# Odd attention: probabilities times values in three passes of high and low parts, for the second half of the queries and heads 0 to 6

## The chip, the cores and the metric

The kernel runs on one core of a Trainium2 chip. The metric is the time of the whole program on the device, in microseconds (us). The engines are PE (TensorE), DVE (VectorE), ACT (ScalarE), POOL (GpSimd) and SP (SyncE, which issues the DMAs). Each runs its own queue of instructions in order and waits for the others through semaphores.

## What is computed

Three transformer layers in float32 over 1024 rows of width 1024. The change is in the second one, the odd layer: an index score keeps at most 256 keys for each query, and 8 heads with 128 columns each (heads 0 to 3 share one set of keys and values, 4 to 7 the other) attend to them:

```python
def dsa_attention(q, k, v, qi, ki, wi, rel_bias):
    ...
        _, idx = lax.top_k(score, topk)
        ...
        logits = jnp.einsum('bqhgd,bqkhd->bqhgk', q_blk, k_sel) * (Dh ** -0.5)
        logits = jnp.where(valid[:, :, None, None, :], logits + bias, NEG_INF)
        p = jax.nn.softmax(logits, axis=-1).astype(v.dtype)
        return jnp.einsum('bqhgk,bqkhd->bqhgd', p, v_sel)

def odd_layer(hn, rel_bias, w_in, w_out, q_g, k_g):
    ...
    att = dsa_attention(q, k, v, qi, ki, wi, rel_bias)
    return (att * jax.nn.silu(gate)) @ w_out
```

The kernel gathers nothing: it computes all logits up to the diagonal and adds a mask of 0 and -1e30.

## The kernel before

All large products are made from parts. A float32 tile x has a high part, x rounded to the type float32r by an ACT copy (`act_panel`, `act_parts`), and a low part, x minus the high one, by a subtraction on POOL or DVE. `mm3` issues three matmuls: high by high, high by low, low by high. Products that are not split are one plain float32 matmul (`mm`); the trace records each of these as two.

The odd layer goes in this order: projections (`qi`, `ki`, `ok`, `ov`, `oq`), the search for the 256th score on DVE and ACT, the eight gate projections `og0` to `og7` with the norms of the heads beside them, then the attention, then the product with `w_out` (`oo`). Weights come in panels of 128 x 1024: SP loads one into one of two raw buffers, ACT makes the high part in one of four slots (8 KB for high and low together), POOL the low part. Panel i+2 is loaded when panel i is split. Before the attention four `oo` panels (oo000 to oo003) are split, one behind each of og4 to og7, and two more lie in the raw buffers.

The attention has 64 units (n, b): head n, query block b of 128 rows with b+1 key blocks. One loop on each engine runs over steps i with shifted stages:

- `s0` on POOL (L2568) adds the bias strip of the head to the mask for b of 2 and more, into one of two tiles by the parity of b. It waits for `od_L` of two blocks earlier.
- `s1` on PE makes the logits (3 or 6 matmuls), DVE (L2318, recorded as CUSTOM_DVE) adds the bias and takes the row minimum of the negated sum (`od_L`), ACT (L2501) takes the exponential with its row sum (`od_exp`).
- `s2`, two steps later: PE turns the 128 x 128 blocks (L267) into a bank of the ring `od_ptb`, up to four blocks a bank, so one bank for b of 0 to 3 and two for b of 4 to 7. A copy moves each bank to the tile `pts[Q]`, where Q is 0 for b below 4 and 1 from 4 on. For b = 4 to 6 ACT (L2510) copies the first bank and DVE (L2333) the second; for b = 7 DVE copies both. The copy frees the bank. The ring has three banks, and each turn needs the bank of three turns ago.
- `s3`, four steps after b = 3 or 7: PE spreads the reciprocals of the row sums (4 matmuls) into a bank of the same ring, then multiplies the values `VN` (stationary) by `pts[Q]` into bank 3. DVE (L2341, L2344) multiplies by reciprocals and gate, ACT (L445) makes the high part of the result and POOL (L2573) the low one.

While a head's Q = 1 probabilities are turned, PE and DVE already work on b = 0 to 3 of the next head: in the order of every engine, the logits, the minimum and the exponential of the next head's b = 0 stand between the copies of b = 5 and of b = 6, and those of b = 1 between b = 6 and b = 7. POOL also makes the low parts of the next head's queries (`query_low`, L2551) at b = 5 and 6. The work around attention's end is: SP waits for the end marks of all engines, reads back the residual of 4 MB and three rows of parameters, and goes on with the panels.

In the kernel, `at` names the semaphore value of an event and `up` raises it.

Of the kernel before, what the change touches and what calls it, by code (L numbers as in the profile page):

```python
# [161 lines left out]
class K:  # L162
# [3 lines left out]
    def __init__(self, nc, d, known):  # L166
# [1656 lines left out]
class Odd:  # L1823


    def __init__(self, k, E):
# [126 lines left out]
def tensor_odd(k, O):  # L1953
# [145 lines left out]
    def s3(n, Q):  # L2099
# [12 lines left out]
        else:  # L2112
            pe.wait_ge(*at("od_g", *before((n, Q), 1, 2)))
        kv, last = n // 4, 4 * Q + 3
        for j in range(last + 1):
            q0 = max(0, j - 4 * Q)
            ins = k.mm(k.bank(3)[:, 128 * q0:512], O.VN[:, j, 128 * kv:128 * kv + 128],
                       O.pts[Q][:, j, q0:4, :].rearrange("p q s -> p (q s)"), j == 0, j == last)
        ins.then_inc(*up("od_O", n, Q))
# [29 lines left out]
def vector_odd(k, O):  # L2149
# [175 lines left out]
    def s2(n, b):  # L2325
        for j0 in range(0, b + 1, 4):
            if j0 == 0 and b % 4 != 3:
                continue
            nj = min(4, b + 1 - j0)
            dve.wait_ge(*at("od_PT_ps", n, b, j0))  # L2330
# [43 lines left out]
def scalar_odd(k, O):  # L2374
# [104 lines left out]
    for m in range(8):  # L2479
        for half in range(2):  # L2480
# [5 lines left out]
            if m >= 2:  # L2486
                act.wait_ge(*at("og_out", m - 2))
            A.activation(O.gev[m % 2][:, 512 * half:512 * half + 512], k.bank(O.proj[("og", m, half)]), ACT.Silu).then_inc(
                *up("og", m, half, also=[("free", "od_proj", "og", m, half)]))
        act_panel(k, PANEL_AT[f"og{m}"] + 4)  # L2490
        if m == 3:
# [10 lines left out]

    def s2(n, b):
        if b % 4 == 3:
            return
# [12 lines left out]
    for i in range(len(O.units) + 4):  # L2518
# [8 lines left out]
        if i < len(O.units) and O.units[i] == (1, 4):  # L2527
            key_high(1)
    k.mark("od_att")
    scalar_out(k, "oo", k.H, "ln0", lambda: act_transposes(k, k.second.x0, "xs", None, (0,)), lambda: k.marks(act, "od_att"))  # L2530
# [3 lines left out]
def pool_odd(k, O):  # L2534
# [13 lines left out]
    def query_low(n, half):  # L2548
        o = slice(512 * half, 512 * half + 512)
        pool.wait_ge(*at("od_qh", n))  # L2550
        G.tensor_tensor(O.QL[:, n, o], O.QT[:, n, o], O.qh[n % 2][:, o].bitcast(F32), ALU.subtract).then_inc(*up("od_ql", n, half))  # L2551

    for name in panels[:-1]:
        pool_panel(k, PANEL_AT[name] + 4)
        if name in ("og4", "og5"):
            key_low(0, int(name == "og5"))
        if name == "og6":
            query_low(0, 0)
            query_low(0, 1)
# [15 lines left out]
    for i in range(4):  # L2575
        s0(*O.units[i])
    pool_panel(k, PANEL_AT[panels[-1]] + 4)
    for i in range(len(O.units) + 7):
        if 4 <= i + 1 < len(O.units):
            s0(*O.units[i + 1])  # L2580
# [13 lines left out]
def sync_odd(k, O):  # L2594
# [37 lines left out]
    for m in range(8):  # L2632
        if m < 7:
            sp_panel(k, PANEL_AT[f"og{m}"] + 6)
        sp.wait_ge(*at("og", m, 1))
        S.dma_start(d["gscr"][128 * m:128 * m + 128], O.gev[m % 2]).then_inc(*up(f"og_out{m % 2}", by=16, also=[("og_out", m)]))
    load_strip(1)
    sp.wait_ge(*at("og_ps", 7, 1))
    load_gate(0)
    sp_panel(k, PANEL_AT["og7"] + 6)  # L2640
    for n, b in O.units:
        if 0 < n < 7 and b == 0:
            load_strip(n + 1)
        if n < 7 and b == 5:
            load_gate(n + 1)
    k.marks(sp, "od_att")
    for t in range(2):
# [1328 lines left out]
```

## Time and profile before

| | us |
|---|---|
| median of three timed runs | 1995.52 (1995.45 to 1996.81) |
| the profiled execution | 1991.9 |
| its span in the trace | 1990.6 |
| attention in the trace, from the first logits to the last product | 810 to 979 |

The profile has a page of totals, and views of the trace: groups of instructions by line and form, waits, a timeline, and busy time in stretches. A record's time is from start to end; matmuls overlap, so their rate is read from the distance between starts or from a count in a stretch. What stands in square brackets behind a record is the idle time of the engine before it and the instruction that ended it.

### The profile page before, as it was taken

To read this page: it belongs to the slowest core of one execution; us is meant where nothing else is said; L and a number is where in the kernel's file an instruction comes from. 1 tells how busy PE (TensorE), PEld (TensorE's weight loads), DVE (VectorE), ACT (ScalarE), POOL (GpSimd) and SP (SyncE) were. 2 spreads that over 40 slices of the span, in tenths; PEclk is the share of its full clock that TensorE was granted. 3 is DMA by queue.
4 is the path that set the end of the run, shared out by engine and by line. 5 is a ranking of instruction groups with operands and counts; after the bars stand their busy time and mean duration, and the time that the engine had idled before them with its cause. 6 is when DMAs were issued, how large, how long until landed. Compare 5 with 4: busy or idle time off the path is not lost.

```text
span 1990.6 us, 24260 instructions
## 1 busy us (share of the span) xinstructions
PE 1924.6 (97%) x9188; PEld 1511.5 (76%) x9188; DVE 1423.6 (72%) x2190; ACT 862.2 (43%) x1457; POOL 640.1 (32%) x453
## 2 busy tenths in 40 slices
PE   7999989999999999999999999999999999999997
PEld 6778766787648787777788777888787877777886
DVE  7668776523279998455356799899999877685549
ACT  5343385333356862555312333444225554352431
POOL 3554410462201222676454000000003663236444
PEclk9999999999999999999999999999999999999999
DMA  7322340442511122211233211121123223455322
GB/s 274 126 74 79 100 146 22 169 149 81 140 35 33 43 85 85 85 65 43 104 119 117 75 39 58 53 64 53 64 97 131 90 75 143 159 193 203 109 91 108
DMA packets 72429, 197.92 MB, mean 99 GB/s; under 512 B 11182, under 2 KB 20559, under 8 KB 71800
## 3 DMA queue, kind: packets, MB, share of 16 engines
q1 hardware_dynamic: 72168, 196.36, 28.9%
q8 instruction: 73, 1.20, 0.2%
q14 instruction: 44, 0.36, 0.1%
q10 hardware_dynamic: 144, 0.00, 0.0%
HBM read 152.90 MB, written 46.71 MB: 100 GB/s over the span
## 4 chain that ended last, share of the span: by engine, by line
PE 54%; DVE 25%; ACT 4%; issue 3%; DMA 1%; POOL 1%; SPq 0%; DVEq 0%; ACTq 0%
PE psum L264 50%; DVE m L3031 6%; DVE m L2194 4%; PE psum L267 3%; DVE m L3052 2%; DVE m L319 1%; DMA m<-in_w 1%; DVE m L3233 1%; ACT m L299 1%; DVE m L532 1%; DVE m L541 1%; DVE m L3170 1%; POOL m L309 1%; DVE m L2263 0%; DVE m L404 0%
## 5 line engine op out<-in xcount | busy, mean ns | idle before, releaser
L264 PE MATMUL psum<-m,m 128*128 128x512 f32 (+8 forms) x8388 | 1844.4, 389 | 38.1 <-DVE m L319 10.0
L264 PEld LDWEIGHTS psum<-m,m 128*128 128x128 f32 (+4 forms) x8388 | 1427.0, 186 | 429.3 <-issue 118.8
L309 POOL TENSOR_TENSOR m<-m,m 128x1024 fp32r<-128x1024 f32 (+1 forms) x122 | 308.6, 2533 | 1003.8 <-ACT m L299 1003.5
L299 ACT ACTIVATE m<-m 128x1024 fp32r<-128x1024 f32 (+2 forms) x166 | 173.6, 1049 | 356.4 <-PE psum L264 228.5
L3031 DVE SCALAR_TENSOR_TENSOR m<-m,m,m 128x1024 f32<-128x1024 f32 x240 | 311.0, 1297 | 6.3
L267 PE MATMUL psum<-m,m 128*128 128x128 f32 x784 | 112.4, 278 | 15.9 <-ACT m L1451 6.2
L267 PEld LDWEIGHTS psum<-m,m 128*128 128x128 f32 x784 | 88.7, 141 | 33.0 <-ACT m L1451 8.2
L2194 DVE TENSOR_SCALAR_CACHE_REDUCE m<-m,m 128x896 bf16<-128x896 f32 (+4 forms) x130 | 102.8, 848 | 1.1
L2568 POOL TENSOR_TENSOR m<-m,m 128x384 f32<-128x384 f32 (+5 forms) x48 | 72.8, 1532 | 43.2 <-DVE m L2318 43.1
L2318 DVE CUSTOM_DVE_ANT_0 m<-psum,m 128x128 f32<-128x128 f32 (+3 forms) x64 | 48.3, 755 | 40.0 <-PE psum L264 22.0
L2414 ACT ACTIVATE m<-m,m 128x1024 bf16<-128x1024 f32 (+1 forms) x62 | 64.1, 1036 | 26.4 <-DVE m L2221 26.4
L319 DVE TENSOR_TENSOR m<-m,m 128x1024 fp32r<-128x1024 f32 (+1 forms) x44 | 52.7, 1198 | 26.0 <-ACT m L299 26.0
L2501 ACT ACTIVATE m<-m,m 128x128 f32<-128x128 f32 (+3 forms) x64 | 49.5, 773 | 37.3 <-DVE m L2318 37.0
L483 DVE TENSOR_TENSOR m<-psum,m 128x512 f32<-128x512 f32 x32 | 21.6, 682 | 60.7 <-PE psum L264 53.9
L2173 DVE SCALAR_TENSOR_TENSOR m<-m,m,m 128x512 f32<-128x512 f32 (+3 forms) x70 | 48.9, 706 | 17.6 <-ACT m L2464 12.9
L2464 ACT ACTIVATE m<-psum 128x512 f32<-128x512 f32 (+3 forms) x80 | 37.7, 522 | 30.2 <-PE psum L264 25.5
L467 POOL TENSOR_TENSOR m<-m,m 128x1 f32<-128x1 f32 x23 | 31.5, 1373 | 50.6 <-DVE m L460 50.6
L3052 DVE SCALAR_TENSOR_TENSOR m<-m,m,m 128x1024 f32<-128x1024 f32 x36 | 46.2, 1283 | 0.9
L404 DVE SCALAR_TENSOR_TENSOR m<-psum,m 128x512 fp32r<-128x512 f32 x32 | 19.7, 681 | 34.1 <-ACT m L393 34.0
L404 DVE SCALAR_TENSOR_TENSOR m<-psum,m,m 128x512 fp32r<-128x512 f32 x32 | 21.6, 743 | 30.8 <-ACT m L393 30.8
L1264 DVE TENSOR_TENSOR m<-psum,m 128x512 f32<-128x512 f32 x16 | 11.0, 689 | 43.3 <-PE psum L264 43.3
L541 DVE SCALAR_TENSOR_TENSOR m<-m,m,m 128x1024 f32<-128x1024 f32 (+1 forms) x25 | 36.8, 1494 | 6.8 <-POOL m L467 6.6
(319 smaller groups left out, 1612.2 us busy)
## 6 DMA issues: line engine op xcount, KB each, us to landing
m<-in_w SPq DMA_DIRECT2D x164, 512.0 KB, 3.5
scr_hscr<-m SPq DMA_DIRECT2D x4, 2048.0 KB, 6.7
m<-scr_hscr SPq DMA_DIRECT2D x4, 2048.0 KB, 10.7
scr_turned<-scr_strip SPq DMA_DIRECT2D x8, 575.5 KB, 13.0
m<-in_x SPq DMA_DIRECT2D x4, 1024.0 KB, 8.1
scr_gscr<-m SPq DMA_DIRECT2D x16, 256.0 KB, 4.2
m<-in_x SPq DMA_DIRECT2D x2, 2048.0 KB, 7.9
m<-scr_turned SPq DMA_DIRECT2D x8, 512.0 KB, 4.5
```

The source lines that it names most:

```text
L264: return self.nc.tensor.matmul(out, lhsT, rhs, start=start, stop=stop, skip_group_check=True)
L267: return self.nc.tensor.transpose(out, in_, self.ident[:, :])
L299: k.nc.scalar.activation(k.hi[SLOT[i]][:, 0:kk * n], k.raw[i % 2][:, 0:kk * n], ACT.Copy).then_inc(*k.up("w_hi", i))
L309: k.nc.gpsimd.tensor_tensor(lo, raw, hi.bitcast(F32), ALU.subtract).then_inc(*k.up("w_lo", i))
L319: k.nc.vector.tensor_tensor(lo, raw, hi.bitcast(F32), ALU.subtract).then_inc(*k.up("w_lo", i))
L541: k.nc.vector.scalar_tensor_tensor(x[:, b, cols], x[:, b, cols], scale, shift[:, cols], ALU.mult, ALU.add).then_inc(*k.up(f"{name}_y", b, ...
L2194: V.tensor_scalar(O.JK[b], O.SC[b], TF[:, c:c + 1] if i else 0.0, None, how, ALU.add, accum_out=CNT[:, c:c + 1]).then_inc(*up("count", i, b))
L2414: A.activation(O.JK[b], O.SC[b], ACT.Sign, bias=O.TB.bitcast(F32)[:, c:c + 1] if i else 0.0, accum_out=O.CNT[:, c:c + 1]).then_inc(*up("si ...
L2501: A.activation(p, p, ACT.Exp, bias=sm[:, 0:1], scale=-1.0, accum_out=O.sums[b // 4][:, b % 4:b % 4 + 1]).then_inc(*up("od_exp", n, b))
L2568: G.tensor_tensor(O.bms[b % 2][:, 0:nk], O.strips[n % 2][:, 1024 - nk:1024], O.MK[:, O.mo[b]:O.mo[b] + nk], ALU.add).then_inc(*up("od_bm", ...
L3031: V.scalar_tensor_tensor(o, u[:, j:j + 1024], w[:, j:j + 1], o, ALU.mult, ALU.add).then_inc(*up("cv_tap", m, j))
L3052: V.scalar_tensor_tensor(o, x[:, j:j + 1024], cw[:, j:j + 1], o, ALU.mult, ALU.add).then_inc(*up("xb_tap", i, j))
```

## The change

For Q = 1 and n below 7 (`parted`), the product of probabilities and values is made by `mm3` from high and low parts in place of one float32 matmul for each key block. For n = 7, and for Q = 0 everywhere, nothing changes.

- Probabilities: for these 28 units ACT copies both banks into a high tile `PTH`, and DVE subtracts that from the same bank into low tiles `PTL`. A bank is free when DVE's subtraction is done.
- Values: ACT makes `VH` in two instructions behind og4's second gate half, POOL makes `VL` in two, one before `query_low` of head 0 and one after the first two bias tiles.
- `VH`, `VL` and the two `PTL` tiles lie in the four weight slots (8 KB each). So the panels oo000 to oo003 are no longer split before the attention. ACT splits them in steps 60, 61, 66 and 67, POOL in steps 63, 64, 66 and 68, and SP loads oo002 to oo005 at the end of the attention, before the residual.

```diff
+        self.PTH = k.tile(X0 + 8 * KB, [8, 4, 128], F32R)
+        slot = [k.slots[SLOT[PANEL_AT[f"oo00{i}"]]] for i in range(4)]
+        self.VH, self.VL = (k.tile(o, [8, 256], F32R) for o in slot[0:2])
+        self.PTL = [k.tile(o, [4, 4, 128], F32R) for o in slot[2:4]]
+        self.parted = lambda n, Q: Q == 1 and n < 7
...
+        if O.parted(n, Q):
+            pe.wait_ge(*at("od_vl"))
         for j in range(last + 1):
...
+            if O.parted(n, Q):
+                parts = (x[:, i, q0:4, :].rearrange("p q s -> p (q s)") for x, i in ((O.PTH, j), (O.PTL[j // 4], j % 4)))
+                ins = k.mm3(out, (O.VH[:, j, hs], O.VL[:, j, hs]), tuple(parts), j == 0, j == last)
+            else:
+                ins = k.mm(out, O.VN[:, j, hs], O.pts[Q][:, j, q0:4, :].rearrange("p q s -> p (q s)"), j == 0, j == last)
...
     def s2(n, b):
         for j0 in range(0, b + 1, 4):
+            nj = min(4, b + 1 - j0)
+            if O.parted(n, b // 4):
+                dve.wait_ge(*at("od_PT_high", n, b, j0))
+                V.tensor_tensor(O.PTL[j0 // 4][:, 0:nj, b % 4, :], k.bank(O.ptb[("PT", n, b, j0)])[:, 0:128 * nj].rearrange("p (j q) -> p j q", j=nj),
+                                O.PTH[:, j0:j0 + nj, b % 4, :].bitcast(F32), ALU.subtract).then_inc(
+                    *up("od_PT_low", n, b, j0, also=[("od_PT", n, b, j0), ("free", "od_ptb", "PT", n, b, j0)]))
+                continue
...
-        act_panel(k, PANEL_AT[f"og{m}"] + 4)
+        if m < 4:
+            act_panel(k, PANEL_AT[f"og{m}"] + 4)
+        if m == 4:
+            act.wait_ge(*at(*done("og4")))
+            for q in range(2):
+                A.activation(O.VH[:, 4 * q:4 * q + 4, :], O.VN[:, 4 * q:4 * q + 4, :], ACT.Copy).then_inc(*up("od_vh", q))
...
+        if O.parted(n, b // 4):
+            for j0 in (0, 4):
+                nj = min(4, b + 1 - j0)
+                act.wait_ge(*at("od_PT_ps", n, b, j0))
+                if n:
+                    act.wait_ge(*at("od_O", n - 1, 1))
+                A.activation(O.PTH[:, j0:j0 + nj, b % 4, :], k.bank(O.ptb[("PT", n, b, j0)])[:, 0:128 * nj].rearrange("p (j q) -> p j q", j=nj), ACT.Copy).then_inc(
+                    *up("od_PT_high", n, b, j0))
+            return
...
+        if i in (60, 61, 66, 67):
+            act.wait_ge(*at("od_O", 6, 1))
+            act_panel(k, PANEL_AT["oo000"] + (60, 61, 66, 67).index(i))
...
+    def value_low(q):
+        b = slice(4 * q, 4 * q + 4)
+        pool.wait_ge(*at(*done("og5")))
+        pool.wait_ge(*at("od_vh", q))
+        G.tensor_tensor(O.VL[:, b, :], O.VN[:, b, :], O.VH[:, b, :].bitcast(F32), ALU.subtract).then_inc(*up("od_vl", "part", q, also=[("od_vl",)] if q else ()))
...
+        if i in (63, 64, 66, 68):
+            pool_panel(k, PANEL_AT["oo000"] + (63, 64, 66, 68).index(i))
```

ACT's order in the attention, from b = 7's exponential of head 3 to the next head's b = 2. m_194 to m_196 hold probabilities, m_198 is `pts[1]`, 128x4x128 is a bank with four blocks. Before:

```order
L2501 ACTIVATE m_196,m_61<-m_196,m_61 128x1024
L2510 ACTIVATE m_198<-psum 128x4x128
L445 ACTIVATE m_201<-m_199 128x512
L2501 ACTIVATE m_194,m_61<-m_194,m_61 128x128
L2510 ACTIVATE m_198<-psum 128x4x128
L2501 ACTIVATE m_195,m_61<-m_195,m_61 128x256
L2501 ACTIVATE m_196,m_61<-m_196,m_61 128x384
```

ACT at the same place after; m_199 is `PTH`:

```order
L2525 ACTIVATE m_195,m_61<-m_195,m_61 128x1024
L2534 ACTIVATE m_199<-psum 128x4x128
L2534 ACTIVATE m_199<-psum 128x2x128
L446 ACTIVATE m_206<-m_205 128x512
L2525 ACTIVATE m_196,m_61<-m_196,m_61 128x128
L2534 ACTIVATE m_199<-psum 128x4x128
L2534 ACTIVATE m_199<-psum 128x3x128
L2525 ACTIVATE m_194,m_61<-m_194,m_61 128x256
L2534 ACTIVATE m_199<-psum 128x4x128 x2
L2525 ACTIVATE m_195,m_61<-m_195,m_61 128x384
```

ACT copies both banks of b = 5, 6 and 7 now, four copies more in this piece.

DVE's order over the same steps; "ISA" with a long tile is the minimum (`od_L`). Before, m_198 being `pts[1]`:

```order
L2344 TENSOR_TENSOR m_199<-psum,m_199 128x512
L2333 COPY m_198<-psum 128x2x128
L2318 ISA m_196,m_61<-psum,m_193 128x128
L2318 ISA m_61 128x1
L2323 RECIPROCAL m_61<-m_61 128x4
L2333 COPY m_198<-psum 128x3x128
L2318 ISA m_194,m_61<-psum,m_193 128x256
L2318 ISA m_61 128x1
L2333 COPY m_198<-psum 128x4x128 x2
```

DVE after, where m_202 and m_203 are the two `PTL` tiles, each written from the bank and `PTH`:

```order
L2343 TENSOR_TENSOR m_202<-psum,m_199 128x4x128
L2343 TENSOR_TENSOR m_203<-psum,m_199 128x2x128
L2331 ISA m_196,m_61<-psum,m_193 128x128
L2331 ISA m_61 128x1
L2336 RECIPROCAL m_61<-m_61 128x4
L2343 TENSOR_TENSOR m_202<-psum,m_199 128x4x128
L2343 TENSOR_TENSOR m_203<-psum,m_199 128x3x128
L2331 ISA m_194,m_61<-psum,m_193 128x256
L2331 ISA m_61 128x1
L2343 TENSOR_TENSOR m_202<-psum,m_199 128x4x128
L2343 TENSOR_TENSOR m_203<-psum,m_199 128x4x128
```

The subtractions of both banks of a block stand ahead of the next head's minimum, and each of them needs ACT's copy.

POOL's order around the start of the attention. L2546 is `key_low`, L2551 `query_low`, L2568 the bias tiles. Before:

```order
L309 TENSOR_TENSOR m_73<-m_65,m_69 128x1024
L2546 TENSOR_TENSOR m_204<-m_155,m_207 128x512
L309 TENSOR_TENSOR m_70<-m_64,m_66 128x1024
L2546 TENSOR_TENSOR m_204<-m_155,m_207 128x512
L309 TENSOR_TENSOR m_71<-m_65,m_67 128x1024
L2551 TENSOR_TENSOR m_203<-m_154,m_205 128x512 x2
L2568 TENSOR_TENSOR m_190<-m_192,m_157 128x384
L2568 TENSOR_TENSOR m_191<-m_192,m_157 128x512
L309 TENSOR_TENSOR m_72<-m_64,m_68 128x1024
```

POOL after, from the panel og7 on (m_72 here); L2593 is `value_low`:

```order
L310 TENSOR_TENSOR m_72<-m_64,m_68 128x1024
L2582 TENSOR_TENSOR m_209<-m_155,m_212 128x512 x2
L2593 TENSOR_TENSOR m_201<-m_156,m_200 128x1024
L2587 TENSOR_TENSOR m_208<-m_154,m_210 128x512 x2
L2613 TENSOR_TENSOR m_190<-m_192,m_157 128x384
L2613 TENSOR_TENSOR m_191<-m_192,m_157 128x512
L2593 TENSOR_TENSOR m_201<-m_156,m_200 128x1024
```

Four panels have left the piece, two `value_low` are new, and the two `key_low` now follow og7's panel at once.

## Rows read from the trace of the kernel before

**Rows 1.** The page: busy time, share of the span, instructions.

```profile
PE 1924.6 (97%) x9188; PEld 1511.5 (76%) x9188; DVE 1423.6 (72%) x2190; ACT 862.2 (43%) x1457; POOL 640.1 (32%) x453
```

**Rows 2.** Stretches: from:to, length, PE, PEld, DVE, ACT, POOL busy (instructions), clock, DMA, GB/s.

```profile
898.78:919.25 20.47, 20.42 (x114) 15.63 (x113) 11.73 (x28) 11.19 (x25) 13.99 (x10) 1.00 0.14 52
...
980.00:1000.00 20.00, 20.00 (x87) 16.11 (x86) 1.38 (x2) 2.75 (x3) 6.08 (x3) 1.00 0.83 326
```

**Rows 3.** PE in one Q = 1 product: its largest form; starts of two weight loads.

```profile
L264 PE MATMUL psum<-m,m 128*128 128x512 f32 x10 | 4.5, 593 | 0.0
...
893.73 0.19 PEld L264 LDWEIGHTS psum<-m,m 128*128 128x128 f32 x1 [0.24 <-issue]
...
894.16 0.19 PEld L264 LDWEIGHTS psum<-m,m 128*128 128x128 f32 x1 [0.24 <-issue]
```

**Rows 4.** Timeline in head 3, bias tile and minimum: start, length, engine, instruction, idle.

```profile
883.97 2.14 POOL L2568 TENSOR_TENSOR m<-m,m 128x1024 f32<-128x1024 f32 x1
...
886.15 1.22 DVE L2318 CUSTOM_DVE_ANT_0 m<-psum,m 128x1024 f32<-128x1024 f32 x1 [1.87 <-POOL m L2568]
```

**Rows 5.** Timeline of the same head, from the copy of b = 5 on.

```profile
888.57 0.57 ACT L2510 ACTIVATE m<-psum 128x512 f32<-128x512 f32 x1
...
888.96 0.28 DVE L2318 CUSTOM_DVE_ANT_0 m<-psum,m 128x128 f32<-128x128 f32 x1
889.04 0.62 ACT L445 ACTIVATE m<-m 128x512 fp32r<-128x512 f32 x1
...
889.56 0.39 ACT L2501 ACTIVATE m<-m,m 128x128 f32<-128x128 f32 x1
...
890.58 0.42 PEld L267 LDWEIGHTS psum<-m,m 128*128 128x128 f32 x4 [0.28 <-ACT m L2510]
...
890.71 0.51 ACT L2501 ACTIVATE m<-m,m 128x256 f32<-128x256 f32 x1 [0.18 <-DVE m L2318]
...
891.63 7.42 PE L264 MATMUL psum<-m,m 128*128 128x512 f32 x27
```

**Rows 6.** Groups by form in one head (878.3 to 898.8): count, busy, mean ns.

```profile
L2341 DVE TENSOR_TENSOR m<-psum,m 128x512 f32<-128x512 f32 x2 | 1.4, 688 | 0.1
...
L2333 DVE COPY m<-psum 128x384 f32<-128x384 f32 x1 | 0.6, 558 | 0.4 <-PE psum L267 0.4
...
L2318 DVE CUSTOM_DVE_ANT_0 m<-psum,m 128x256 f32<-128x256 f32 x1 | 0.4, 414 | 0.0
```

**Rows 7.** Timeline before the attention: DVE's mask work, POOL beside it, PE's gate products.

```profile
771.34 1.15 DVE L2266 SCALAR_TENSOR_TENSOR m<-m,m,m 128x896 f32<-128x896 f32 x1
772.53 3.17 DVE L2268 SCALAR_TENSOR_TENSOR m<-m,m,m 128x896 f32<-128x896 f32 x1
775.74 1.58 DVE L2270 TENSOR_SCALAR m<-m 128x896 bf16<-128x896 f32 x1
...
771.87 2.88 POOL L309 TENSOR_TENSOR m<-m,m 128x1024 fp32r<-128x1024 f32 x1 [9.45 <-ACT m L299]
774.71 2.12 POOL L2546 TENSOR_TENSOR m<-m,m 128x512 fp32r<-128x512 f32 x1
...
778.78 6.16 PE L264 MATMUL psum<-m,m 128*128 128x512 f32 x26 [2.64 <-DVE m L2281]
786.45 25.03 PE L264 MATMUL psum<-m,m 128*128 128x512 f32 x111 [1.52 <-DVE m L2281]
```

**Rows 8.** Timeline at the start of the attention: ACT's last panel, PE's first turn.

```profile
810.44 1.05 ACT L299 ACTIVATE m<-m 128x1024 fp32r<-128x1024 f32 x1
...
813.35 0.33 PE L267 MATMUL psum<-m,m 128*128 128x128 f32 x1 [1.87 <-ACT m L2501]
```

**Rows 9.** Timeline behind the attention: the residual's load and its first reader.

```profile
982.11 0.92 SPq L2648 DMA_DIRECT2D m<-scr_hscr  x2
...
997.41 0.69 DVE L483 TENSOR_TENSOR m<-psum,m 128x512 f32<-128x512 f32 x1 [17.43 <-PE psum L264]
```

**Rows 10.** The page's DMA issues: KB each, median us to landing.

```profile
m<-scr_hscr SPq DMA_DIRECT2D x4, 2048.0 KB, 10.7
```

More of the change, by code:

```diff
@@ L195, in __init__ @@
         place = [8 * KB * (3 if i == LENT else i - (i > LENT)) for i in range(4)]
+        self.slots = [self.R0 + 8 * KB + place[i] for i in range(4)]
         self.hi = [self.tile(self.R0 + 8 * KB + place[i], [1024], F32R) for i in range(4)]
@@ L2114, in s3 @@
         kv, last = n // 4, 4 * Q + 3
+        hs = slice(128 * kv, 128 * kv + 128)
+        if O.parted(n, Q):
+            pe.wait_ge(*at("od_vl"))
         for j in range(last + 1):
             q0 = max(0, j - 4 * Q)
-            ins = k.mm(k.bank(3)[:, 128 * q0:512], O.VN[:, j, 128 * kv:128 * kv + 128],
-                       O.pts[Q][:, j, q0:4, :].rearrange("p q s -> p (q s)"), j == 0, j == last)
+            out = k.bank(3)[:, 128 * q0:512]
+            if O.parted(n, Q):
[3 more added lines that the diff above has]
+                ins = k.mm(out, O.VN[:, j, hs], O.pts[Q][:, j, q0:4, :].rearrange("p q s -> p (q s)"), j == 0, j == last)
         ins.then_inc(*up("od_O", n, Q))
@@ L2326, in s2 @@
         for j0 in range(0, b + 1, 4):
+            nj = min(4, b + 1 - j0)
[5 more added lines that the diff above has]
+                continue
             if j0 == 0 and b % 4 != 3:
                 continue
-            nj = min(4, b + 1 - j0)
             dve.wait_ge(*at("od_PT_ps", n, b, j0))
@@ L2551, in query_low @@
         G.tensor_tensor(O.QL[:, n, o], O.QT[:, n, o], O.qh[n % 2][:, o].bitcast(F32), ALU.subtract).then_inc(*up("od_ql", n, half))
+    def value_low(q):
[3 more added lines that the diff above has]
+        G.tensor_tensor(O.VL[:, b, :], O.VN[:, b, :], O.VH[:, b, :].bitcast(F32), ALU.subtract).then_inc(*up("od_vl", "part", q, also=[("od_vl",)] if q else ()))
     for name in panels[:-1]:
-        pool_panel(k, PANEL_AT[name] + 4)
+        if name not in ("og4", "og5", "og6"):
+            pool_panel(k, PANEL_AT[name] + 4)
         if name in ("og4", "og5"):
             key_low(0, int(name == "og5"))
+        if name == "og5":
+            value_low(0)
         if name == "og6":
@@ L2576, in pool_odd @@
         s0(*O.units[i])
-    pool_panel(k, PANEL_AT[panels[-1]] + 4)
+    value_low(1)
     for i in range(len(O.units) + 7):
+        if i in (63, 64, 66, 68):
+            pool_panel(k, PANEL_AT["oo000"] + (63, 64, 66, 68).index(i))
         if 4 <= i + 1 < len(O.units):
@@ L2632, in sync_odd @@
     for m in range(8):
-        if m < 7:
+        if m < 4:
             sp_panel(k, PANEL_AT[f"og{m}"] + 6)
@@ L2639, in sync_odd @@
     load_gate(0)
-    sp_panel(k, PANEL_AT["og7"] + 6)
     for n, b in O.units:
@@ L2645, in sync_odd @@
             load_gate(n + 1)
+    for i in range(2, 6):
+        sp_panel(k, PANEL_AT["oo000"] + i)
     k.marks(sp, "od_att")
```

## Prediction

> **What bounds the kernel now.** I read the page first: PE is busy 97% of the span [rows 1], so work taken off PE is worth its time where PE is dense. Then the stretches: one head of the attention takes 20.47 us, and PE is busy in 20.42 of them, DVE in 11.7, ACT in 11.2, POOL in 14.0 [rows 2]. The other engines have room on average. What they have room for at one place is another question, and the timeline of one head answers it [rows 4, 5]: PE turns the blocks b = 5, 6 and 7 of a head within some 3.5 us, through a ring of three banks, and waits there 0.28 us already for an ACT copy [rows 5].
>
> **The product itself.** Eight float32 matmuls leave each of seven heads. They are recorded as two passes each; passes of 512 columns start 0.43 us apart [rows 3], and I take the same rate per column for the narrow ones: 10 of 512 columns, 2 of 384, 2 of 256, 2 of 128, so 4.30 + 0.64 + 0.43 + 0.22 = 5.59 us. The matmuls of three passes run, in a dense stretch, at 87 in 20 us, 0.23 us for 512 columns [rows 2]. The new product has 15 of those, and three each of 384, 256 and 128 columns, at 0.17, 0.115 and 0.11 us by the same rate (the last bounded by its weight load): 3.45 + 1.19 = 4.64 us. That is 0.95 us less for a head, 6.6 us for seven.
>
> The Trainium skill, page "TensorE: Matmul & The Clock Gate", section "Back-to-back issue gap", gives a distance of N/2.4 + 2.5 ns, 216 ns for 512 columns. By it the saving would be 1.16 us a head and the end 1.5 us earlier. The trace does not agree, with 230 ns, and the trace is used.
>
> **The parts of the probabilities.** For 28 units ACT gains the second bank's copy (two for b = 7), 128 to 512 columns, 2.3 us a head, and DVE's copies become subtractions of every bank, 2.1 us a head more (the three first banks of 512 columns at 0.69 [rows 6]). A subtraction reads a bank and a tile as L2341 does, so I take 0.69 us for 512 columns, and for 384 the 0.56 of the copy [rows 6]. By totals both engines stay near 14 of 20 us. By order they do not hide, since bank after bank now goes from ACT to DVE before it is free, and between b = 5, 6 and 7 stand the next head's minimum on DVE and exponential on ACT, each waiting for the other.
>
> I lay this out on head 3's own clock. ACT comes free for b = 5's first bank at 888.57 [rows 5], and no earlier: ahead of it lies b = 7's exponential, ahead of that the minimum at 886.15, which waits 1.87 us for POOL's tile [rows 4]. POOL's tile for b = 6, the low part of the queries and the tile for b = 7 come one after another behind b = 4's minimum, and that behind the previous product. So the start of the piece keeps its distance from the previous product, and everything from here adds up:
>
> - ACT's high part of (5, first bank) 888.57 to 889.14; DVE's two low parts 889.17 to 890.2. The next head's minimum for b = 0 starts at 890.11 in place of 888.96, its exponential at 890.44 in place of 889.56 [rows 5].
> - High parts of b = 6 890.83 to 891.77 (0.47 from start to start, as from 888.57 to 889.04 [rows 5]); low parts 891.43 to 892.60. Minimum for b = 1 (0.41 [rows 6]) at 892.52, exponential at 892.98 in place of 890.71 [rows 5].
> - High parts of b = 7 893.49 to 894.54; low parts 894.10 to 894.79 and to 895.40.
> - PE: the second bank of b = 6 waits for the low part of b = 5's first (889.86), b = 7's second bank for b = 6's first (892.12). The four reciprocal matmuls need b = 7's first bank, so they start near 894.85. Before they started at 892.4: the group of 27 at 891.63 holds three logit matmuls of 0.23 us ahead of them [rows 5].
>
> The product starts 2.5 us later in its head and takes 0.95 less: **+1.55 us a head**. Afterwards nothing is owed: during the product DVE, ACT and POOL have over 4 us for the next head's b = 2 and 3. Heads 1 to 6 pay this in full, 9.3 us.
>
> What the delay could be at least and at most: if every handover took nothing, the piece would still have the ACT and DVE instructions in series that the list shows, which leaves about 1.9 of the 2.5 us (nine handovers and two of PE at 0.03 to 0.05 taken out); if a handover costs 0.1 us more than the 0.03 to 0.05 that I use, at nine handovers, it is 3.4. Per head that is +0.95 to +2.45.
>
> **The start.** Four panels leave ACT (1.05 us each [rows 8]) and POOL before the attention. At the last one ACT's first exponential is held, and PE waits 1.87 us [rows 8]; without it 0.9 us of that goes. POOL loses a panel in front of head 0's bias tiles, worth 1.0 us in its chain. Head 0 then pays 2.5 - 0.95 - 1.0 = +0.6 us.
>
> Further ahead, DVE's mask work bounds PE, which waits 2.64 and 1.52 us for it [rows 7]. L2268 takes 3.17 us beside POOL's panel at 771.87 where L2266, with the same shape, takes 1.15 [rows 7], and L2270 takes 1.58 beside L2546, about 0.95 more than its size asks. This collision of 3.0 us goes, since that panel goes, and PE would follow. But the two `key_low` move up behind og7's panel, where DVE does the same kind of work for b = 6. They can cost 0.75 us (one instruction held) to 2.4 (two held, the scan L2263 among them). No row shows the scan beside POOL, so I take the middle, 1.6, nearer to neither: **-1.4 us**, between -2.3 and -0.6.
>
> The Trainium skill, "SBUF — State Buffer", on the shared port pair, says that a DVE instruction with two SBUF inputs and a POOL instruction lock each other out for a whole instruction. L2268 beside POOL agrees. The scan has two SBUF inputs as well, and by that rule the 2.4 would hold and the whole kernel come out 0.8 us later than my sum.
>
> The value parts cost two ACT copies and two POOL subtractions where both are idle, covered by the gate projections on PE (25 us without a wait [rows 7]). Uncovered they would be 2.1 and 4.8 us once.
>
> **The end.** Panels oo000 and oo001 are split on ACT in gaps between exponentials; the exponential of b = 7 moves by 0.7 us, and PE turns that block over a microsecond later. POOL splits the four one after another behind its last bias tile. The fourth stands between the high and the low part of head 7's last result: ACT's copy of 1.05 us [rows 8] and POOL's 2.4 us (2.88 in a collision [rows 7]), so POOL's end mark, and with it SP's load of the residual, comes some 3.3 us later than 982.11 [rows 9]. The first reader waited for PE at 997.41 [rows 9], with the load issued 15 us before; the median landing is 10.7 us [rows 10], so it is covered with about 1 us left, and behind that reader PE has banks enough for 20 us. PE uses a panel in 24 x 0.23 = 5.5 us, so it needs the last of the four over 16 us after the first. I take nothing. Without the cover it is 3 us.
>
> **Sum.** -1.4 + 0.6 + 9.3 = +8.5 us. The profiled execution took 1991.9 us, 3.6 less than the median of the timed runs; the sum is made on its trace and laid on the median: 1995.5 + 8.5 = **2004 us**.
>
> **Rivals.**
> 1. *Half a relay.* The handovers overlap more than I lay out (ACT's copy runs ahead of the minimum, banks come back sooner), and a head's delay is about the saving, 0.5 to 1.3 us. For it: the engines' totals. Against it: program order on DVE and ACT. Time: 1995.5 - 1.4 - 1, plus up to 6 x 0.4, so 1993 to 1997.
> 2. *Faster: no relay.* PE never waits, because the piece's start is not pinned to POOL and drifts ahead head by head. It decides at a delay below 0.5 us a head. Against it: the minimum's wait of 1.87 us for POOL [rows 4]. Time: 1995.5 - 6.6 - 1.4 - 0.9 = 1986.6.
> 3. *A dearer relay and a bare end.* Handovers 0.1 us dearer (+0.9 x 6) and the residual's 3 us uncovered: 2012.
> 4. *The lock rule* on the scan: 2005, inside the forecast.
>
> **Chances.** Forecast with the lock rule, 1999.5 to 2010: 0.66. Rival 1: 0.14. Rival 2: 0.08. Rival 3: 0.12, of which half lies above 2011. The range of 8 in 10 goes from 1996 to 2011. A difference of 0.2%, 4 us, is about what a measurement of this kernel can tell from none. Faster by more than that: 0.09 (rival 2 and a little of rival 1). Within it: 0.14. Slower: 0.77.
>
> **What would show it.** The trace after should have 24 matmuls in the product, 4.6 to 4.7 us long; the head's period at 22.0 us; PE idle in front of the reciprocals and between the turns of b = 6 and 7, ended by DVE's subtraction; PE's restart near 785 in place of 786.45; no new idle time of PE behind 980. The prediction is wrong if the period is under 21 us, if b = 5's first high part comes earlier after the previous product than 10.3 us, or if subtractions take other than 0.69 us.

## The result, and the profile after

| | before | after |
|---|---|---|
| median of the timed runs, us | 1996.16 (1995.45 to 1997.47, 4 runs) | 2008.71 (2007.12 to 2011.07, 4 runs) |
| ratio, 95% interval | | 1.0065 (1.005 to 1.0079) |
| the profiled execution, us | 1991.9 | 2009.41 |
| its span; mean granted clock | 1990.6; 0.996 | 2007.0; 0.991 |

The change makes the kernel 12.5 us slower. Forecast were 2004 us and a range of 1996 to 2011. A second series gave 2008.71 us again (5 runs), with a ratio of 1.0066.

The page's busy line, to be held against [rows 1]: PE has work for 4 us more and a smaller share.

```profile
PE 1929.0 (96%) x9244; PEld 1525.5 (76%) x9244; DVE 1436.4 (72%) x2211; ACT 877.9 (44%) x1494; POOL 647.1 (32%) x455
```

One head in stretches, with the columns of [rows 2]: it takes 22.45 us in place of 20.47, and PE is busy in 19.75 of them.

```profile
910.03:932.48 22.45, 19.75 (x123) 16.68 (x122) 13.39 (x31) 13.10 (x30) 14.04 (x10) 1.00 0.14 47
```

The waits of the same head say who holds whom: engine and line, what it waited for, us in total, times, the longest.

```profile
DVE m L2343 <- ACT m L2534: 4.3, 4, 1.7
...
PEld psum L268 <- DVE m L2343: 2.5, 2, 1.3
...
PE psum L268 <- DVE m L2343: 2.0, 2, 1.1
PEld psum L265 <- DVE m L2343: 1.1, 1, 1.1
```

ACT holds DVE and DVE holds PE three times: twice at the turns (L268), once at the reciprocals. Before, PE's weight loads waited twice in this piece for an ACT copy, 0.20 us (at 889.19) and the 0.28 us in [rows 5].

The timeline of the piece in that head, 31.76 us later than head 3 of before. It starts with b = 4's parts and b = 7's minimum (L2331), which answers to [rows 4]; the rest answers to [rows 5]. L2534 is ACT's high part, L2343 DVE's subtraction, L2525 the exponential.

```profile
915.35 2.13 POOL L2613 TENSOR_TENSOR m<-m,m 128x1024 f32<-128x1024 f32 x1
...
917.12 0.89 DVE L2343 TENSOR_TENSOR m<-psum,m 128x512 fp32r<-128x512 f32 x2 [1.68 <-ACT m L2534]
...
917.93 1.21 DVE L2331 CUSTOM_DVE_ANT_0 m<-psum,m 128x1024 f32<-128x1024 f32 x1
...
920.33 0.85 ACT L2534 ACTIVATE m<-psum 128x512 fp32r<-128x512 f32 x2
920.94 1.02 DVE L2343 TENSOR_TENSOR m<-psum,m 128x512 fp32r<-128x512 f32 x2 [0.46 <-ACT m L2534]
...
921.69 0.55 PE L268 MATMUL psum<-m,m 128*128 128x128 f32 x3 [1.10 <-DVE m L2343]
...
921.88 0.28 DVE L2331 CUSTOM_DVE_ANT_0 m<-psum,m 128x128 f32<-128x128 f32 x1
...
922.20 0.40 ACT L2525 ACTIVATE m<-m,m 128x128 f32<-128x128 f32 x1 [0.50 <-DVE m L2331]
...
922.60 0.96 ACT L2534 ACTIVATE m<-psum 128x512 fp32r<-128x512 f32 x2
923.21 1.16 DVE L2343 TENSOR_TENSOR m<-psum,m 128x512 fp32r<-128x512 f32 x2 [0.96 <-ACT m L2534]
923.96 0.66 PE L268 MATMUL psum<-m,m 128*128 128x128 f32 x4 [0.94 <-DVE m L2343]
924.29 0.41 DVE L2331 CUSTOM_DVE_ANT_0 m<-psum,m 128x256 f32<-128x256 f32 x1
...
924.74 0.51 ACT L2525 ACTIVATE m<-m,m 128x256 f32<-128x256 f32 x1 [1.18 <-DVE m L2331]
...
925.25 1.06 ACT L2534 ACTIVATE m<-psum 128x512 fp32r<-128x512 f32 x2
925.86 1.29 DVE L2343 TENSOR_TENSOR m<-psum,m 128x512 fp32r<-128x512 f32 x2 [1.15 <-ACT m L2534]
926.61 5.77 PE L265 MATMUL psum<-m,m 128*128 128x128 f32 x32 [0.66 <-DVE m L2343]
```

Read it as a chain: high part, subtraction, minimum, exponential, high part, and so on. Each of them starts behind the one above, because it needs its result or stands behind it in its engine's order. Laid beside the prediction's list with 31.76 taken off, every start of ACT and DVE from b = 5's high part to b = 7's agrees within 0.02 us, and so do the reciprocals on PE: the minimum of b = 0 at 890.12 (forecast 890.11), its exponential at 890.44 (890.44), the high parts of b = 6 at 890.84 (890.83), those of b = 7 at 893.49 (893.49), the reciprocals at 894.85 (894.85).

What the prediction did not have stands at the top. The subtraction of b = 4 waits 1.68 us for ACT, and b = 7's minimum is queued behind it. POOL's tile is ready at 917.48, the minimum starts at 917.93. Before, nothing of DVE stood there, and the minimum started 0.04 us after the tile ended [rows 4].

The start and the end of the attention:

```profile
767.16 4.32 POOL L2582 TENSOR_TENSOR m<-m,m 128x512 fp32r<-128x512 f32 x2
767.66 2.73 DVE L2276 TENSOR_TENSOR_SCAN m<-m,m 128x768 f32<-128x768 f32 x1
770.42 1.87 DVE L2279 SCALAR_TENSOR_TENSOR m<-m,m,m 128x768 f32<-128x768 f32 x1
...
775.41 6.15 PE L265 MATMUL psum<-m,m 128*128 128x512 f32 x26 [0.41 <-DVE m L2294]
...
782.41 6.14 PE L265 MATMUL psum<-m,m 128*128 128x512 f32 x26 [0.86 <-DVE m L2294]
...
1002.96 0.93 SPq L2696 DMA_DIRECT2D m<-scr_hscr  x2
...
1014.98 0.69 DVE L484 TENSOR_TENSOR m<-psum,m 128x512 f32<-128x512 f32 x1 [17.44 <-PE psum L265]
```

The collision of 3 us in [rows 7] is gone, and the two `key_low` (L2582) now hold two DVE instructions of an earlier block. The same two in the kernel before:

```profile
762.88 1.76 DVE L2263 TENSOR_TENSOR_SCAN m<-m,m 128x768 f32<-128x768 f32 x1
764.67 1.02 DVE L2266 SCALAR_TENSOR_TENSOR m<-m,m,m 128x768 f32<-128x768 f32 x1
```

At the end, the residual's load is issued later, and its first reader still waits for PE for as long as before, 17.44 us against 17.43 [rows 9]: the end costs nothing.

### The profile page after: what moved, and what is told of

Read it like the earlier page. It is cut to its first block, busy times and chain, and to the rows that moved or that the text cites. A ratio compares the mean times of both kernels' runs of the same rounds, so it can differ in the third digit from the quotient of the medians.

```text
span 2007.0 us, 24460 instructions
## 1 busy us (share of the span) xinstructions
PE 1929.0 (96%) x9244; PEld 1525.5 (76%) x9244; DVE 1436.4 (72%) x2211; ACT 877.9 (44%) x1494; POOL 647.1 (32%) x455
## 4 chain that ended last, share of the span: by engine, by line
PE 55%; DVE 23%; ACT 4%; issue 3%; DMA 1%; POOL 1%; SPq 0%; DVEq 0%; ACTq 0%
PE psum L265 53%; DVE m L2207 4%; DVE m L3079 3%; PE psum L268 2%; DVE m L3100 1%; ACT m L2525 1%; DVE m L2331 1%; DVE m L2343 1%; DVE m L320 1%; DVE m L3281 1%; DMA m<-in_w 1%; ACT m L2534 1%; DVE m L533 1%; ACT m L300 1%; DVE m L2276 1%
## 5 line engine op out<-in xcount | busy, mean ns | idle before, releaser
L265 PEld LDWEIGHTS psum<-m,m 128*128 128x128 f32 (+3 forms) x8444 | 1439.6, 186 | 419.6 <-issue 103.6
L268 PE MATMUL psum<-m,m 128*128 128x128 f32 x784 | 115.1, 282 | 27.6 <-DVE m L2343 13.5
L268 PEld LDWEIGHTS psum<-m,m 128*128 128x128 f32 x784 | 89.9, 143 | 45.0 <-DVE m L2343 17.0
L2525 ACT ACTIVATE m<-m,m 128x128 f32<-128x128 f32 (+3 forms) x64 | 49.5, 774 | 48.6 <-DVE m L2331 48.4
L2331 DVE CUSTOM_DVE_ANT_0 m<-psum,m 128x128 f32<-128x128 f32 (+3 forms) x64 | 47.7, 753 | 23.7 <-PE psum L265 19.4
L2343 DVE TENSOR_TENSOR m<-psum,m 128x512 fp32r<-128x512 f32 (+3 forms) x56 | 30.5, 586 | 29.8 <-ACT m L2534 29.8
## 6 DMA issues: line engine op xcount, KB each, us to landing
scr_turned<-scr_strip SPq DMA_DIRECT2D x8, 575.5 KB, 12.5
```

Of the source, the lines that this page charges most:

```text
L265: return self.nc.tensor.matmul(out, lhsT, rhs, start=start, stop=stop, skip_group_check=True)
L268: return self.nc.tensor.transpose(out, in_, self.ident[:, :])
L2331: V.tensor_tensor_reduce(out=p, in0=k.bank(O.pairs[b % 2], 2)[:, 0:nk], in1=win, scale=-1.0, scalar=3e38, op0=ALU.add, op1=ALU.min, accum_ ...
L2525: A.activation(p, p, ACT.Exp, bias=sm[:, 0:1], scale=-1.0, accum_out=O.sums[b // 4][:, b % 4:b % 4 + 1]).then_inc(*up("od_exp", n, b))
```

## Experiments

Each ratio is against the kernel before on the same chip. One thing has to be known to compare them. PE's granted clock falls to half for 3.4 us at some places of every traced execution, and their number varies, so that a run's mean clock lies between 0.987 and 0.997. Over all 123 timed runs here, within each series, 0.001 of mean clock goes with 1.17 us. The table gives each kernel's time at a clock of 0.993 by this fit, beside the period of a head without such a fall, read between DVE's last gate products (L2363). A time at 0.993 is uncertain by 0.2 us for the kernel before and by 0.3 to 0.9 us for the others.

| kernel | runs | median, us | ratio (95%) | mean clock | at 0.993 | period, us |
|---|---|---|---|---|---|---|
| before, beside the kernels below | 49 | 1994.2 to 1995.9 | 1 | 0.9931 to 0.9941 | 1994.9 to 1995.8 | 20.47 |
| after, two series | 9 | 2008.7 | 1.0065, 1.0066 | 0.9908 | 2006 | 22.46 |
| relay_only | 4 | 2011.9 | 1.009 (1.0075 to 1.0105) | 0.9925 | 2011.3 | 23.42 |
| product_only | 4 | 1985.7 | 0.9958 (0.9943 to 0.9973) | 0.9937 | 1986.4 | 19.53 |
| panels_only | 10 | 1992.8 | 0.999 (0.998 to 1.0) | 0.9932 | 1993.0 | 20.47 |
| b4_first | 5 | 2001.8 | 1.0033 (1.002 to 1.0046) | 0.9950 | 2003.9 | 22.17 |
| b4_again | 5 | 2004.1 | 1.0052 (1.0033 to 1.0071) | 0.9928 | 2005.6 | 22.17 |
| min_first | 4 | 2004.3 | 1.0062 (1.0042 to 1.0082) | 0.9905 | 2002.1 | 21.41 |
| both_orders | 11 | 2000.0 | 1.0026 (1.0016 to 1.0036) | 0.9915 | 1998.9 | 21.10 |
| relay_order | 11 | 1992.1 | 0.9986 (0.9974 to 0.9997) | 0.9928 | 1992.3 | 20.10 |
| relay_late4 | 11 | 1992.2 | 0.9986 (0.9977 to 0.9995) | 0.9940 | 1992.6 | 20.40 |

**The relay without the cheaper product.**

```diff
-                ins = k.mm3(out, (O.VH[:, j, hs], O.VL[:, j, hs]), tuple(parts), j == 0, j == last)
+                ins = k.mm(out, O.VN[:, j, hs], next(parts).bitcast(F32), j == 0, j == last)
```

> The changed kernel with its way of making the parts (ACT's high part, DVE's subtraction, bank freed by it) but with the product as it was, one float32 matmul for each key block, from the values VN and the high tile PTH. The low parts of the probabilities are made and not read, and so are the value parts. My theory: the product saves 0.95 us a head and everything else of the 12.5 us is the relay and what stands ahead of it, so this kernel is the changed one plus 7 x 0.95: 2015.3 us, ratio to the kernel before 1.0096, product of 27 float32 matmuls 5.6 us long again, period of a head 23.4 us. Rival A (the three-pass product is itself what costs, because its 24 matmuls with their weight loads and low tiles disturb PE or its clock): back to 1996 to 2000 us. Rival B (the saving of the product is not on the path because PE waits behind it anyway): no change against the changed kernel, 2008.7 us.

2011.9 us, and a period of 23.42 against 22.46: the product's 0.96 us a head come back, as forecast. Rivals A and B fall. The median is 3.4 us below what was expected, of which 2 us go with the higher clock.

**The cheaper product without the relay.** DVE, and ACT likewise, copy straight to `PTH`. The product reads `PTH` where it would read `PTL`, so the kernel leaves out the low part of the probabilities:

```diff
-                V.tensor_tensor(O.PTL[j0 // 4][:, 0:nj, b % 4, :], ..., ALU.subtract)
+                V.tensor_copy(O.PTH[:, j0:j0 + nj, b % 4, :], k.bank(...)...)
```

> The changed kernel with the three-pass product and the value parts, but the probabilities copied as in the kernel before: one copy of each bank, straight to PTH, by ACT for the first bank and DVE for the second (DVE both for b = 7), bank freed by that copy. The low part of the probabilities is left out; PTH is read in its place, so the number of matmuls and their shapes are those of the changed kernel. My theory: no relay, so -6.6 us for seven products and -2.1 us at the start: 1987.5 us, ratio 0.9956, period of a head 19.5 us. Rival A (the three-pass product costs by itself): 1996 us or more, period 20.5 or more. Rival B (the piece is pinned to POOL, so that 0.95 us saved behind it come back as a wait for a bias tile): about 1994 us, period 20.4 us, with more idle time of DVE in front of b = 7's minimum.

1985.7 us. A head of it in stretches; PE is dense again, with the 123 matmuls of the changed kernel:

```profile
897.14:916.68 19.54, 19.50 (x123) 16.78 (x122) 11.74 (x29) 11.20 (x25) 14.06 (x10) 1.00 0.16 55
```

20.47 less 19.54 is 0.93 us, and the time is 1.8 us lower than expected. So the product was worth what the sum gave it, and the relay takes 22.46 - 19.53 = 2.93 us a head. Rivals A and B fall.

**The panels moved, nothing else.**

```diff
-        self.parted = lambda n, Q: Q == 1 and n < 7
+        self.parted = lambda n, Q: False
```

> The changed kernel with the copies and the product of the kernel before, but with the four panels moved to the end of the attention and the value parts made (and not read). My theory: the start gives 2.1 us and POOL's chain in head 0 up to 1.0 more, the end is covered and costs nothing, the period stays 20.5 us: 1993.1 to 1994.1 us, ratio 0.9985 to 0.999, first turn of the attention 2.1 us nearer to the search's end than before. Rival A (the end is bare): 1996 to 1997 us, with PE idle behind 980. Rival B (part of the loss seen in the changed kernel, the 4.8 us that its trace is behind at 770 us, where no instruction is changed, belongs to the program's layout and not to one run): 1998 us, with the shift present at 770 us.

1992.8 us, at equal clock about 2 us under before. In the trace PE is 1.5 us behind the kernel before at 660 us and 0.55 ahead of it at its first turn (813 us), 2.1 us gained, and keeps this through all eight heads. Rival A falls. Rival B falls too: the shift at 770 us in the changed kernel's first trace is made of falls of the clock in unchanged code, at 304, 386 and 652 us, and is another from trace to trace (1.5 us here).

**The changed kernel again.**

> The changed kernel once more, nothing edited, to see which part of its time belongs to the program and which to one execution. In its first trace PE's clock was at half rate for 3.4 us at seven places, three of them in the attention, against two places in the kernel before. My theory: the period of a head is 22.45 us wherever no such stretch falls, and the half-clock stretches lie elsewhere this time, with 0 to 3 in the attention; the shift at 770 us, where no instruction is changed, is another than 4.8 us. Rival (they belong to PE's new idle times of 1.1 us before the turns): the same three in the attention at the same instructions, and heads of 23.1 to 23.4 us again.

Undisturbed heads are of 22.46 to 22.48 us again. The shift in unchanged code, read at 660 us, is 2.8 us this time, against 4.8. (The first trace has eight falls before the program's end, not seven: at 293, 304, 386, 652, 833, 877, 969 and 1252 us.) In the attention the clock falls twice, at 827.7 and 943.8 us, where it fell at 832.7, 877.0 and 969.2 us in the first trace. The rival, the same three again, falls. Yet the places are not arbitrary either (see the last section).

**b = 4's high parts earlier on ACT.**

```diff
+        early = turned is not None and turned[1] == 4 and turned[0] < 7
+        if early:
+            s2(*turned)
         if i < len(O.units):
             s1(*O.units[i])
-        if 2 <= i <= len(O.units) + 1:
-            s2(*O.units[i - 2])
+        if turned and not early:
+            s2(*turned)
```

> The changed kernel, but ACT makes the high parts of b = 4 ahead of the exponential of b = 6 instead of behind it. Nothing left out. My theory: in the trace of the changed kernel DVE waits 1.68 us for these high parts, and b = 7's minimum, which is next on DVE, starts 0.45 us after POOL's tile is ready; with the edit it starts when the tile is there, the period is 22.0 us in place of 22.45 (in the head after head 1, where POOL is late anyway, nothing changes), and the time falls by 6 x 0.45 = 2.7 us. Rival (b = 7's minimum is set by something else, or the exponential of b = 6, now 0.75 us later, holds PE's turn of b = 6 as much): period 22.45 as before, no gain.

The mechanism holds, the size was 0.30 in place of 0.45 us: the minimum waits for POOL now, and starts 0.13 us after the tile's end (911.02), where it was 0.04 before the change [rows 4]. This 0.1 us stands in front of b = 7's minimum in every head with a relay where POOL's tile comes last, in whatever order the relay is, and neither in head 7 nor in product_only and panels_only (0.03 us there). What makes it is open.

```profile
908.89 2.13 POOL L2617 TENSOR_TENSOR m<-m,m 128x1024 f32<-128x1024 f32 x1
...
911.15 1.23 DVE L2331 CUSTOM_DVE_ANT_0 m<-psum,m 128x1024 f32<-128x1024 f32 x1 [1.38 <-POOL m L2617]
```

Five heads of 0.3 us are 1.5 us, yet the median fell by 6.9. The same kernel was run again for that:

> The kernel of b4_first once more, unedited. Its periods and the changed kernel's account for 0.9 us between the two (five heads of 22.17 in place of 22.46, a sixth equal but for a half-clock stretch), and their medians were 6.9 us apart, with mean granted clocks of 0.995 and 0.991. Theory A (the clock level goes with the kernel, for reasons other than the waits in the attention, which are the same in both): again 0.994 to 0.996, and 2001 to 2003 us. Theory B (it goes with the session or the single execution): a mean clock of 0.991 to 0.993 this time and 2004 to 2007 us.

Its clock came out at 0.9928 and its time at 2004.1 us, as theory B has it: the kernel alone doesn't fix the clock. At equal clock the two series are 2.1 and 0.4 us below the changed kernel; the periods say 1.5.

**The next head's minima earlier on DVE.** `s2` for b = 5 and 6 comes a step later:

```diff
-            s2(*O.units[i - 2])
+            n, b = O.units[i - 2]
+            if n < 7 and b in (6, 7):
+                s2(n, b - 1)
+            if n == 7 or b not in (5, 6):
+                s2(n, b)
```

> The changed kernel with another order on DVE: the next head's minimum for b = 0 stands ahead of the two subtractions of b = 5, and that for b = 1 ahead of those of b = 6, so that the subtractions of b = 5, 6 and 7 come one block later in DVE's order. Same instructions, nothing left out. My theory (the loss is the alternation of ACT's high part, DVE's subtraction, DVE's minimum and ACT's exponential, each behind the other): laid out on head 3's clock the product starts 0.75 us later than before the change in place of 2.5, so -1.75 us a head: -12 us with head 0, 1996.5 us, ratio 1.0002, period 20.7 us. Rival (the loss is the work itself, ACT's and DVE's added instructions in the piece, whatever their order, or a bank freed too late): no gain or a loss, 2007 to 2012 us, with PE's wait for a bank growing as the subtractions move back.

A miss. The period is 21.4 us, 1.05 us less a head in place of 1.75, and the time is 2004.3 us where 1996.5 were expected; 2.2 us of that are the low clock. The rival (no gain, PE's wait for a bank growing) falls by the period. The trace names what came late instead:

```profile
918.14 0.55 PE L268 MATMUL psum<-m,m 128*128 128x128 f32 x3 [1.12 <-DVE m L2343]
...
918.44 0.60 PE L265 MATMUL psum<-m,m 128*128 128x256 f32 x3
...
919.19 0.42 DVE L2331 CUSTOM_DVE_ANT_0 m<-psum,m 128x256 f32<-128x256 f32 x1 [0.77 <-PE psum L265]
```

The logits of b = 1 (918.44) stand on PE behind the turn of b = 6's second bank, and that waits for the bank of b = 5. My layout had followed ACT and DVE and not PE's order. I put the minimum ahead of a subtraction that could have run, and DVE stood for 0.77 us.

**Both edits.**

> The edits of b4_first and of min_first together. min_first alone measured a period of 21.4 us in undisturbed heads, where I had expected 20.7: DVE's minimum for b = 1 waited 0.77 us for PE's logits, which stand behind PE's turn of b = 6's second bank, and that behind the bank of b = 5. My theory: the two edits act at different places and add up, period 20.95 us, so 0.5 us a head more than in the kernel before, -2 us at the start: 1996 to 1998 us, ratio 1.000 to 1.001. Rival (with the minimum of b = 7 earlier, another wait, POOL's tile or the bank, takes its place): period stays at 21.4, 1999 to 2001 us.

Period 21.10 us, 0.31 less than min_first alone: they add up (0.29 and 1.05 alone, 1.36 together). 20.95 was expected, and 1996 to 1998 us; 2000.0 us came out, of which 1 us goes with the clock. By its time alone the rival would stand, by the period it falls.

**An order for the relay.** On ACT the high parts of b = 6 and 7 go ahead of the next head's exponentials, on DVE only the minimum of b = 0 goes ahead of b = 5's subtractions:

```diff
+            if n < 7 and b == 6:
+                s2(n, 5)
+            if n == 7 or b != 5:
+                s2(n, b)
...
-        early = turned is not None and turned[1] == 4 and turned[0] < 7
+        early = turned is not None and turned[1] in (4, 6, 7) and turned[0] < 7
...
+            if turned[1] == 7:
+                s3(turned[0], 0)
```

> As b4_first, and further: ACT makes the high parts of b = 6 ahead of the next head's exponential for b = 0 and those of b = 7 ahead of the one for b = 1, with the copy L446 behind them; DVE does the next head's minimum for b = 0, then the subtractions of b = 5 and 6, then the minimum for b = 1, then the subtractions of b = 7. Nothing left out. My theory (the loss is only the order, since ACT and DVE have the time): high parts follow one another without the exponentials between them, DVE is then busy without a wait from b = 5's subtraction to b = 7's first, 0.7 + 0.35 + 1.15 + 0.4 + 0.7 = 3.3 us, the product starts 0.9 us earlier than in min_first, the period is 20.0 to 20.2 us, below the 20.47 of the kernel before: 1990 to 1993 us, ratio 0.998. Rival (the ring of three banks, each now freed after two steps, is the limit whatever the order): period 20.9 or more, 1996 us or more.

Period 20.10 us, 1992.1 us: 16.6 us less than the changed kernel (13.7 at equal clock) by order alone, and 0.14% under the kernel before. Most of these 0.14% comes with the panels: panels_only, with the old copies and the old product, comes to 1993.0 us at equal clock against 1992.3 here, and from the first turn to the last gate product its trace is 0.9 us the longer. So the relay, in the best order tried, still takes most of what the cheaper product gives (6.6 us in the sum). The piece in one head, b = 5's high part at 909.56:

```profile
909.56 1.34 ACT L2538 ACTIVATE m<-psum 128x512 fp32r<-128x512 f32 x3
...
910.17 1.62 DVE L2343 TENSOR_TENSOR m<-psum,m 128x512 fp32r<-128x512 f32 x3
...
912.02 0.56 DVE L2343 TENSOR_TENSOR m<-psum,m 128x384 fp32r<-128x384 f32 x1 [0.23 <-ACT m L2538]
...
912.92 1.29 DVE L2343 TENSOR_TENSOR m<-psum,m 128x512 fp32r<-128x512 f32 x2
...
913.08 6.46 PE L265 MATMUL psum<-m,m 128*128 128x512 f32 x35
```

From 910.17 on DVE waits 0.23 us in all, where it waited 0.96 and 1.15 us before. PE's last group, three logit matmuls (0.7 us), the reciprocals and the product without a wait, starts 3.5 us after b = 5's high part; in the changed kernel the reciprocals alone start 6.3 us after it. The rival, that a ring of three banks is the limit in any order, falls; one wait of PE for a bank is left (1.06 us for weights, 0.83 us for matmuls, at 910.91).

**The same without its first edit.**

> The kernel of relay_order without its first edit: ACT makes the high parts of b = 4 behind the exponential of b = 6 again, as in the changed kernel. Theory A (the minimum of b = 7 is held 0.31 us by the subtraction of b = 4, whatever stands behind): period 20.4 us in place of 20.1, 1.6 to 1.9 us more than relay_order, so 1994 us, ratio 0.9993. Theory B (what counts in relay_order is only the piece from b = 5 to 7): period 20.1 and 1992 us.

Period 20.40 us: b = 4's subtraction holds the minimum by 0.30 us here as well, as theory A says and B does not. From the first turn to the last gate product the trace is 1.5 us longer than relay_order's, which is five such heads. The timed runs do not show it (1992.2 against 1992.1, 1992.6 against 1992.3 at equal clock, uncertain by 0.3 and 0.5).

## Why the prediction was right, and where not

The sign, the mechanism and the range were right. By steps, from the two traces of the changed kernel:

- **The product**: forecast 0.95 us a head less. Measured 0.93 (product_only) and 0.96 (relay_only). In the changed kernel it takes 4.7 us.
- **The relay from b = 5 to the product**: forecast 2.5 us, laid out instruction by instruction from rows of before, and right to 0.02 us at each.
- **Its start**: the prediction said "the start of the piece keeps its distance from the previous product". This step failed. The distance was 9.89 us before (from the last gate product L2344 at 878.68 to the high part at 888.57 [rows 5]) and is 10.30 after. (The 10.3 us in the prediction's signs is another distance, from the last matmul of the product; that one went from 10.27 to 10.69.) I had asked what stands ahead of ACT's copy, and followed that to the minimum and to POOL. I had not asked what the change puts in front of that minimum on DVE, which is b = 4's subtraction. The minimum starts 7.90 us after the gate product, at 917.93, and started 7.47 us after it before [rows 4]: 0.43 us a head. By exchange 0.3 us of it is b = 4's subtraction (b4_first, and relay_late4 against relay_order); the other 0.1 is the later start behind POOL's tile, of which the cause is open. The period is 22.46 in place of 22.02. In the head behind head 1 POOL is late anyway and the subtraction costs nothing: there the period went from 21.72 to 23.40, 1.68 for a forecast of 1.55. So heads 1 to 6 cost 11.6 us without falls of the clock, where 9.3 stood in the sum.
- **The start**: DVE's part was forecast at -1.4. The two instructions held by `key_low` take 2.73 and 1.87 us in place of 1.76 and 1.02, 1.8 us more for a forecast of 1.6, with the scan among them. PE's lag behind the kernel before shrinks from 4.79 us at 760 us to 3.64 at its restart, which is 785.3 on the clock of the kernel before (forecast "near 785"), and to 2.69 at the first turn: 2.1 in all, as in panels_only. The price by the lock rule, 2.4, and the middle that was taken, 1.6, lie on either side of the measured 1.8, so no run decides rival 4.
- **Head 0**: forecast +1.55 from its first turn on. Measured +1.8 in the second trace: the lag behind the kernel before goes from 0.71 us at the first turn to 2.53 at the last gate product. A fall of the clock lies in it, at 827.7 in the middle of a wait. In b4_first one lies 0.4 us behind the same wait, b4_again has none, and head 0 takes 24.77 us from its first turn to its last gate product in both, so I count it as free. Start and head 0 together: -0.8 forecast, -0.3 measured.
- **The end**: forecast 0, with the load 3.3 us later in its place. It is issued at 1002.96, which is 3.3 us later than 982.11 moved by the shift of 17.56 us, and is covered.
- **What the sum did not hold**: the clock. By the steps above the change costs -0.3 + 11.6 = +11.3 us. At equal clock the two kernels are 10.2 to 11.1 us apart, uncertain by some 0.6. The rest of the measured 12.5, some 1 to 2 us, goes with the mean clock of 0.9908, where the kernel before has 0.993 to 0.994.

The forecast was 8.5 us and the result 12.5. The start of the piece made 2.3 of the difference (1.5 of it b = 4's subtraction), the start and head 0 made 0.5, and the rest, 1.2, goes with the clock. The range held because it was wide enough for two terms that the sum had at nothing.

None of the prediction's signs of being wrong came: the period is over 21 us, the high part of b = 5 comes later after the product, not earlier, and a subtraction of 512 columns takes 0.69 us. Rivals 1 and 2 fall, since a head's delay is 2.9 us (22.46 less 19.53); rival 3 falls, since the handovers are as laid out and the end is covered. Two figures beside the sum are off: rival 1's terms give 1993 to 1995.5 and not 1997, and the 1.16 us given beside the saving of 0.95 changes only the terms of 512 columns, not the narrower ones.

## What to carry to other kernels

Where a copy by one engine is replaced by a copy and a subtraction by two, the price isn't in their totals, which had room to spare here. It is in the program order of both engines: each instruction that stands between two links of the chain, for the sake of other work, becomes a link itself. Lay out such a piece on the trace's own clock with all three engines' orders, PE's too, look for what the change puts ahead of every instruction that others wait for, and then move out of the chain what nobody needs yet. Here that turned a loss of 0.65% into a gain of 0.14% without changing a single instruction; most of that gain comes with moving the panels alone (panels_only).

## What the runs showed of the hardware

In the attention, falls of the clock follow the relay's waits. In the nine traces with the relay PE's clock fell thirteen times inside the attention, each time while PE stood in a wait at a turn (L268) or at most 0.7 us behind it, and that was the second or third such wait of its piece. Most had no fall: these traces hold 63 pieces of the relay, seven each, and b4_again has no fall in any. In the three traces without the relay (before, product_only, panels_only) it never fell there. Stretches of the changed kernel, with the columns of [rows 2], the clock being the last but two:

```profile
921.00:924.40 3.40, 1.78 (x15) 1.54 (x15) 2.44 (x8) 2.06 (x6) 1.28 (x1) 1.00 0.58 225
...
966.00:969.20 3.20, 1.64 (x13) 1.40 (x14) 2.25 (x7) 2.01 (x6) 1.28 (x1) 1.00 0.15 60
969.20:972.60 3.40, 3.40 (x14) 3.02 (x13) 2.25 (x8) 1.57 (x4) 0.00 (x0) 0.50 0.02 5
```

The first row is one head's piece of the relay and the second is another's, alike in PE's work. Behind the second PE runs at 1.2 GHz for 3.4 us, behind the first at 2.4 GHz. Such a fall made its head in the changed kernel 0.6 us longer (23.12 and 23.10 for 22.46), some 0.7 in head 0 (833 us), and nothing in the head at 877 us (23.39, with 23.40 in the second trace without a fall); in min_first it was 1.6 (23.03 and 22.98 for 21.4). In code where PE is dense it costs 1.5 to 1.7 us each time: the first trace falls behind the kernel before by that much at 304, 386 and 652 us. So the falls in the attention are a part of what goes with the clock above. Most of the falls lie in unchanged code outside the attention, at places that repeat from trace to trace (about 293 to 295, 304, 386 and 650 us) but not in every one. Why the changed kernel had the lower clock in both of its series, b4_first the highest and the same kernel a middle one later, no run settles.
